# Remainders of all raw weight slabs by a negative ScalarE copy and an adding DMA, in a two-layer transformer kernel

## What is computed

```python
for i in range(DEPTH):
    x = layer_norm(DN_ALPHA * x + 0.5 * swiglu(x, ffn1_w_gate[i], ffn1_w_up[i], ffn1_w_down[i]), ...)
    y = swa_mixer(...) if kind == 0 else nsa_mixer(...)
    x = layer_norm(DN_ALPHA * x + y, ...)
    x = layer_norm(DN_ALPHA * x + mem_cross_attention(x, mem, ...), ...)
    x = layer_norm(DN_ALPHA * x + 0.5 * swiglu(x, ffn2_w_gate[i], ffn2_w_up[i], ffn2_w_down[i]), ...)
```

## Time and profile before

| | before |
|---|---|
| median of 3 runs | 2184.62 us (2184.2 to 2186.59) |
| profiled execution | 2184.3 us from its first to its last instruction |
| TensorE busy | 2161.4 us (99%) |
| VectorE busy | 1334.5 us (61%) |
| ScalarE busy | 1068.6 us (49%) |
| GpSimd busy | 779.0 us (36%) |
| HBM traffic | 203.10 MB read, 2.10 MB written, 94 GB/s |

### The profile page before, as it was taken

One profiled execution on the slowest core, in us unless ns is written; L12 is line 12 of the kernel. 1 busy time (PEld: TensorE's weight loads), 2 busy tenths in 40 slices (PEclk: granted clock), 3 DMA queues, 4 the chain that ended last, 5 costly groups with the idle time before them and its releaser, 6 DMA issues.

```text
span 2184.3 us, 35402 instructions
## 1 busy us (share of the span) xinstructions
PE 2161.4 (99%) x13640; PEld 1918.4 (88%) x13640; DVE 1334.5 (61%) x2315; ACT 1068.6 (49%) x1927; POOL 779.0 (36%) x573
## 2 busy tenths in 40 slices
PE   9999999999999999999999999999999999999998
PEld 8999998878888989898899999887778887989896
DVE  7656667464436928385766666657655346747475
ACT  4434345563435525254643534466654445535353
POOL 3201116567638030305420111555548555120203
PEclk9999999999999999999999999999999999999999
DMA  4323334213313333333232333320004312333332
GB/s 152 122 93 95 110 113 134 77 49 109 123 39 107 107 97 108 95 110 123 87 118 96 97 107 114 119 79 29 20 11 132 110 49 77 116 97 96 108 97 78
DMA packets 58199, 207.50 MB, mean 95 GB/s; under 512 B 6960, under 2 KB 7088, under 8 KB 57264
## 3 DMA queue, kind: packets, MB, share of 16 engines
q1 hardware_dynamic: 56016, 197.68, 28.9%
q10 hardware_dynamic: 2016, 7.55, 0.9%
HBM read 203.10 MB, written 2.10 MB: 94 GB/s over the span
## 4 chain that ended last, share of the span: by engine, by line
PE 93%; DVE 3%; ACT 1%; POOL 1%; issue 1%; DMA 0%; DVEq 0%; ACTq 0%
PE bank L1772 14%; PE bank L1773 14%; PE bank L1774 14%; PE bank L1983 11%; PE bank L1988 11%; PE bank L1985 11%; PE bank L2184 2%; PE bank L2145 2%; PE bank L2117 1%; PE bank L2118 1%; PE bank L1872 1%; PE bank L1874 1%; PE bank L1873 1%; PE bank L1791 1%; PE bank L1802 1%
## 5 line engine op out<-in xcount | busy, mean ns | idle before, releaser
L627 POOL TENSOR_TENSOR w_lo<-w_raw,w_hi 128x1024 fp32r<-128x1024 f32 (+1 forms) x226 | 530.1, 2354 | 1175.3 <-ACT w_hi L804 1175.2
L1772 PE MATMUL bank<-h_hi,w_hi 128*128 128x512 f32 x960 | 377.8, 394 | 1.5 <-DVE h_lo L1751 0.8
L1773 PE MATMUL bank<-h_lo,w_hi 128*128 128x512 f32 x960 | 374.4, 390 | 0.0
L1774 PE MATMUL bank<-h_hi,w_lo 128*128 128x512 f32 x960 | 373.8, 389 | 0.0
L804 ACT ACTIVATE w_hi<-w_raw 128x1024 fp32r<-128x1024 f32 (+1 forms) x227 | 230.4, 1021 | 130.5 <-PE bank L1774 92.4
L1772 PEld LDWEIGHTS bank<-h_hi,w_hi 128*128 128x128 f32 x960 | 180.3, 188 | 45.5 <-issue 3.3
L1774 PEld LDWEIGHTS bank<-h_hi,w_lo 128*128 128x128 f32 x960 | 180.2, 188 | 38.2
L1773 PEld LDWEIGHTS bank<-h_lo,w_hi 128*128 128x128 f32 x960 | 180.5, 188 | 34.2
L1983 PE MATMUL bank<-x_hi,w_hi 128*128 128x256 f32 x864 | 139.6, 284 | 0.3
L1772 PE MATMUL bank<-x_hi,w_hi 128*128 128x512 f32 x352 | 139.2, 396 | 0.0
L1988 PE MATMUL bank<-x_hi,w_lo 128*128 128x256 f32 x864 | 138.9, 283 | 0.0
(11 more groups left out here) (307 smaller groups left out, 5036.0 us busy)
## 6 DMA issues: line engine op xcount, KB each, us to landing
w_raw<-w_dram SPq DMA_DIRECT2D x315, 512.0 KB, 3.5
w_raw<-w_dram SPq DMA_DIRECT2D x64, 448.0 KB, 3.3
f<-mem_dram ACTq DMA_DIRECT2D x5, 1024.0 KB, 5.2
out_dram<-t SPq DMA_DIRECT2D x8, 256.0 KB, 2.2
t<-x_dram SPq DMA_DIRECT2D x2, 512.0 KB, 6.9
f<-cmp_w_dram ACTq DMA_DIRECT2D x1, 1024.0 KB, 4.9
t<-x_dram ACTq DMA_DIRECT2D x2, 256.0 KB, 5.5
t<-x_dram ACTq DMA_DIRECT2D x1, 512.0 KB, 8.1
```

The costliest lines, as they stand in the source:

```text
L627: pool.tensor_tensor(w_lo[:, slot(s), 0:n * P], w_raw[:, s % RAW, 0:n * P], w_hi[:, slot(s), 0:n * P].bitcast(F32), ALU.subtract).then_inc ...
L1772: pe.matmul(dst, w_hi[:, slot(s), w], m_hi[:, k, :], start=k == 0, stop=False)
L1773: pe.matmul(dst, w_hi[:, slot(s), w], m_lo[:, k, :], start=False, stop=False)
L1774: last = pe.matmul(dst, w_lo[:, slot(s), w], m_hi[:, k, :], start=False, stop=k == n - 1)
```

## The change

ScalarE now writes two copies of a raw slab: the rounded one into w_hi as before, and right behind it one with scale -1 into w_lo, which then holds minus the rounded value. GpSimd issues a DMA that reads the same slab from DRAM a second time and adds it onto w_lo (`accum_op=ALU.add`), so that w_lo ends as the remainder. This replaces GpSimd's subtraction for 226 slabs, and VectorE's `gate_rest` and `up_rest` for the 76 gate slabs and 76 up halves of the Strassen groups. The remainders of sums (`pair_rest`, `late_rest`) and of slab 0 stay with VectorE. neg_ready counts the negative copies; lo_landed (one for each slot), gate_lo and up_lo now count landings, 16 for each. SyncE reloads a raw buffer after the negative copy. To make room for the new semaphores iota_done is merged into pool_set and sinks_neg into dist_ready; their waits (pool_set at 8 and 9, dist_ready at 6) are not all shown.

```diff
         hi_ready = sem("hi_ready")
-        lo_ready = sem("lo_ready")
+        neg_ready = sem("neg_ready")
+        lo_landed = [sem(f"lo_landed{i}") for i in range(SLOTS)]
...
+        row_of = {}
+        for n in set(sizes):
+            for row, s in enumerate([s for s in range(total) if sizes[s] == n]):
+                row_of[s] = row
+
+        def turn_of(s):
+
+            return len([x for x in range(s + 1) if x not in grouped and x not in by_dve and slot(x) == slot(s)])
+
+        turns_of = {s: turn_of(s) for s in range(total)}
...
         def wait_lo(engine, s):
 
-            before = len([x for x in by_dve if x < s])
             if s in by_dve:
-                engine.wait_ge(lo_dve, before + 1)
+                engine.wait_ge(lo_dve, by_dve.index(s) + 1)
             else:
-                engine.wait_ge(lo_ready, plain(s) - before)
+                engine.wait_ge(lo_landed[slot(s)], 16 * turns_of[s])
...
             for s, n in enumerate(sizes):
                 if s >= RAW and s - RAW in grouped:
                     g = grouped[s - RAW]
                     if s - RAW == g.gate:
-                        sp.wait_ge(gate_lo, g.count + 1)
+                        sp.wait_ge(gate_hi, 2 * g.count + 2)
                         sp.wait_ge(wsum_ready, 4 * g.count + 4)
                     else:
                         sp.wait_ge(wsum_ready, 4 * g.count + 2)
-                        sp.wait_ge(up_lo, g.count + 1)
+                        sp.wait_ge(up_hi, 2 * g.count + 2)
+                elif s >= RAW and s - RAW in by_dve:
+                    wait_lo(sp, s - RAW)
                 elif s >= RAW:
-                    wait_lo(sp, s - RAW)
+                    sp.wait_ge(neg_ready, plain(s - RAW) - len([x for x in by_dve if x < s - RAW]))
...
-                sp.dma_start(w_raw[:, s % RAW, 0:n * P], io["w%d" % n][rows[n], :, :]).then_inc(raw_landed[s % RAW], 16)
-                rows[n] += 1
+                sp.dma_start(w_raw[:, s % RAW, 0:n * P], io["w%d" % n][row_of[s], :, :]).then_inc(raw_landed[s % RAW], 16)
...
-                    pool.wait_ge(hi_ready, plain(s))
-                    pool.tensor_tensor(w_lo[:, slot(s), 0:n * P], w_raw[:, s % RAW, 0:n * P],
-                                       w_hi[:, slot(s), 0:n * P].bitcast(F32), ALU.subtract).then_inc(lo_ready, 1)
+                    pool.wait_ge(neg_ready, plain(s) - len([x for x in by_dve if x < s]))
+                    pool.dma_start(w_lo[:, slot(s), 0:n * P], io["w%d" % n][row_of[s], :, :],
+                                   accum_op=ALU.add).then_inc(lo_landed[slot(s)], 16)
...
+            def group_rests(g):
+
+                pool.wait_ge(gate_hi, 2 * g.count + 2)
+                if g.count:
+                    pool.wait_ge(gate_lo, 16 * g.count)
+                pool.dma_start(w_gate(g)[1], io["w8"][row_of[g.gate], :, :], accum_op=ALU.add).then_inc(gate_lo, 16)
+                pool.wait_ge(up_hi, 2 * g.count + 2)
+                if g.count:
+                    pool.wait_ge(up_lo, 16 * g.count)
+                pool.dma_start(w_up(g)[1], io["w8"][row_of[g.up], :, 512:1024], accum_op=ALU.add).then_inc(up_lo, 16)
...
             def ffn(st):
                 feed(st.up[0][WHOLE - 1][1])
                 if st.ln == 0:
                     masks()
                 for part in range(len(FPARTS)):
-                    feed(st.out[part][-1])
+                    for g in st.groups[part]:
+                        if g is not st.groups[0][0] and g is st.groups[part][0]:
+                            feed(st.out[part - 1][-1])
+                        group_rests(g)
+                feed(st.out[-1][-1])
                 if st.ln in MEMORY:
                     memory_split(MEMORY[st.ln])
                 feed(st.out[-1][-1] + 3)
...
@@ -802,6 +826,9 @@
                         act.wait_ge(slab_done, plain(same_slot(s)))
                     after_group(s)
                     act.activation(w_hi[:, slot(s), 0:n * P], w_raw[:, s % RAW, 0:n * P], ACT.Copy).then_inc(hi_ready, 1)
+                    if s not in by_dve:
+                        act.activation(w_lo[:, slot(s), 0:n * P], w_raw[:, s % RAW, 0:n * P], ACT.Copy,
+                                       scale=-1.0).then_inc(neg_ready, 1)
...
                     act.activation(w_gate(g)[0], raw(g.gate), ACT.Copy).then_inc(gate_hi, 1)
+                    act.activation(w_gate(g)[1], raw(g.gate), ACT.Copy, scale=-1.0).then_inc(gate_hi, 1)
...
                     act.activation(w_up(g)[0], raw_half(g.up, 1), ACT.Copy).then_inc(up_hi, 1)
+                    act.activation(w_up(g)[1], raw_half(g.up, 1), ACT.Copy, scale=-1.0).then_inc(up_hi, 1)
...
-            dve.wait_ge(iota_done, 3)
+            dve.wait_ge(pool_set, 8)
...
-                def gate_rest(g):
-
-                    dve.wait_ge(gate_hi, g.count + 1)
-                    hi, lo = w_gate(g)
-                    dve.tensor_tensor(lo, raw(g.gate), hi.bitcast(F32), ALU.subtract).then_inc(gate_lo, 1)
...
-                def up_rest(g):
-                    hi, rest = w_up(g)
-                    dve.wait_ge(up_hi, g.count + 1)
-                    dve.tensor_tensor(rest, raw_half(g.up, 1), hi.bitcast(F32), ALU.subtract).then_inc(up_lo, 1)
...
-                gate_rest(begin)
...
-                gate_rest(begin.next)
-                up_rest(begin)
...
                             sums_second(g.next)
-                            if g is not begin:
-                                gate_rest(g.next)
                             pair_rest(g.next)
...
-                        if g.next:
-                            up_rest(g.next)
...
                         elif after and j == 5:
-                            gate_rest(after)
                             pair_rest(after)
...
-                    if after:
-                        up_rest(after)
...
-                    pe.wait_ge(gate_hi, g.count + 1)
-                    quarter(bank_a(g)[:, 0:256], w_gate(g), 0, x_block(0, 0), True, (gate_lo, g.count + 1), m1)
+                    pe.wait_ge(gate_hi, 2 * g.count + 1)
+                    quarter(bank_a(g)[:, 0:256], w_gate(g), 0, x_block(0, 0), True, (gate_lo, 16 * g.count + 16), m1)
...
-                    quarter(bank_b(g)[:, half[1]], w_gate(g), 1, x_block(1, 0), True, (gate_lo, g.count + 1), m2)
+                    quarter(bank_b(g)[:, half[1]], w_gate(g), 1, x_block(1, 0), True, (gate_lo, 16 * g.count + 16), m2)
...
-                    pe.wait_ge(up_hi, g.count + 1)
+                    pe.wait_ge(up_hi, 2 * g.count + 1)
                     pe.wait_ge(up2_out, g.count + 1)
-                    quarter(bank_b(g)[:, half[0]], w_up(g), 0, comb[4], False, (up_lo, g.count + 1), m4)
```

More of the change, by code:

```diff
@@ L411, in build @@
         pool_set = sem("pool_set")
-        iota_done = sem("iota_done")
         dist_f = sem("dist_f")
@@ L418, in build @@
         cmp_in = sem("cmp_in")
-        sinks_neg = sem("sinks_neg")
         out_done = sem("out_done")
@@ L592, in _ @@
         def _(sp):
-            rows = {7: 0, 8: 0}
             for s, n in enumerate(sizes):
@@ L634, in _ @@
             pool.memset(eps[:], EPS).then_inc(pool_set, 1)
-            pool.iota(dist_i[:, 0:512], [[1, 512]], base=-384, channel_multiplier=-1).then_inc(iota_done, 1)
+            pool.iota(dist_i[:, 0:512], [[1, 512]], base=-384, channel_multiplier=-1).then_inc(pool_set, 1)
             pool.iota(dist_i[:, 512:640].rearrange("p (i n) -> p i n", i=NT), [[-128, NT], [16, 32]], base=0,
-                      channel_multiplier=-1).then_inc(iota_done, 1)
-            pool.iota(dist_i[:, 640:896], [[1, 256]], base=-128, channel_multiplier=-1).then_inc(iota_done, 1)
+                      channel_multiplier=-1).then_inc(pool_set, 1)
+            pool.iota(dist_i[:, 640:896], [[1, 256]], base=-128, channel_multiplier=-1).then_inc(pool_set, 1)
             pool.wait_ge(pool_set, 5)
@@ L655, in masks @@
                 pool.wait_ge(consts_in, 64)
-                pool.tensor_scalar(nsinks[:], sinks[:], -1.0, None, ALU.mult).then_inc(sinks_neg, 1)
+                pool.tensor_scalar(nsinks[:], sinks[:], -1.0, None, ALU.mult).then_inc(dist_ready, 1)
             def base(st, j):
@@ L710, in mixer @@
                     pool.wait_ge(x_ready, KC * (st.ln + 1))
-                    pool.wait_ge(sinks_neg, 1)
+                    pool.wait_ge(dist_ready, 6)
                     for p in range(2):
@@ L1638, in mixer @@
                 if st.kind == "swa":
-                    dve.wait_ge(sinks_neg, 1)
+                    dve.wait_ge(dist_ready, 6)
                 def recip(u):
@@ L1964, in shift @@
             def shift(st):
-                pe.wait_ge(pool_set, 6)
+                pe.wait_ge(pool_set, 9)
                 pe.wait_ge(lead_ready, st.ln + 1)
@@ L2018, in prod4 @@
                         pe.wait_ge(comb_lo, c0 + 3)
-                    pe.wait_ge(up_hi, g.count + 1)
+                    pe.wait_ge(up_hi, 2 * g.count + 1)
```

(2 more changed lines are left out.)

## The result

| | before | after |
|---|---|---|
| median of 4 runs | 2185.61 us (2184.2 to 2187.03) | 2568.14 us (2558.68 to 2579.24) |
| profiled execution | 2184.3 us | 2564.9 us |

The ratio is 1.1753, 95% interval 1.1719 to 1.1786: slower by 382 us. The forecast was 2345 us, 160 us more than before, with a range up to 2540: the sign was right, the size was not.

The account below looks back on a forecast made before the run. TensorE was taken to bound the kernel, so only late w_lo counts: 2184.3 us + 152 of waits + 8 in layer norms = 2344, given as 2345 us against the runs' median; range 2235 to 2540.

Parts of the forecast that it names:

- the named places: Readers of w_lo with too short a gap: first down slabs, tight groups, output, memory and NSA input slabs; 152 us.
- One sign: GpSimd's busy time, listed among what would show the forecast right: POOL near 250 us.
- D = 5.5 us: Issue to landing of a 512 KB adding transfer into w_lo: 5.2 us from mem loads plus 0.3 us issue.
- the lower bound: D bounded from below by a plain 512 KB transfer: 3.5 us median, 3.0 us the fastest.
- the steady groups: The other 48 or so Strassen groups: gap 6.84 us, 0.3 us to spare, so no wait forecast.
- the first rival: Adding transfers land later, so steady groups wait too from D = 5.8 us; 2468 us at D = 7; chance 0.25.
- the sum had 51: Waits at tight Strassen groups: 30 us at first two groups of four stages, 21 at second groups of eight parts.
- the 16 places that the forecast named: Tight Strassen groups: first and second of four stages, second of eight later parts; 2.59 to 3.86 us each.
- 45 + 23 + 21 + 7 + 5 = 101: Waits outside groups: first down slabs 45, output slabs 23, memory pairs 21, NSA inputs 7, other places 5 us.
- rival 3: Waits of 3 to 4 us lower TensorE's clock: 58 us on the forecast, 2403 us; chance 0.12.
- 8 us were allowed: Layer norms: negative copies on ACT between x_hi copies; bounds 0 and 15 us, 8 taken.
- rival 1 at D = 8.1 us: Worst case of late landings: 111 us at 48 groups, 112 at 43 other places; 2570 us, 0.08, outside the range.

Follow-up runs that it names:

- e7: Kernel before, with only the 112 ordinary slabs whose w_hi lies ready 10 us or more taking the new route: 2196.02 us, ratio 1.0049.
- e9: e8 with one wait turned: SyncE reloads a gate's raw buffer when the adding transfer has landed, not after the negative copy: 2266.35 us, ratio 1.0365.
- e4: Changed kernel with plain transfers in place of adding ones, so w_lo holds the slab itself and only time is of use: 2335.7 us, ratio 1.0684.
- e8: Kernel before, with only the groups' gate remainders by negative copy and adding transfer; up halves by DVE, ordinary slabs by POOL: 2362.68 us, ratio 1.0798.
- e10: Changed kernel with SyncE reloading every raw buffer only when the adding transfer of its slab has landed: 2502.4 us, ratio 1.1453.
- e3: Kernel before plus ScalarE's negative copies; POOL and VectorE add w_raw onto them instead of subtracting, no adding transfer: 2231.15 us, ratio 1.0203.

## Why the prediction was wrong

**What bounds the kernel, and where it would hurt: right.** TensorE waits for adding transfers at the named places, and POOL's relief wins nothing that shows (`e7`); DVE's was not tested alone. One sign failed at no cost: POOL is busy for 570.5 us and not near 250, since each of its 378 issues counts 0.86 us.

**D = 5.5 us: right for a transfer alone, wrong for this kernel.** Lone landings took 5.64 us, the freed gates of `e9` 5.4 us. Without the addition a lone landing took 3.8 us (`e4`), between the 3.5 us of the lower bound and D, and over the 3.2 us that the prediction weighed for it. But the transfers are hardly ever alone, and the prediction put crowding into its range only. The step that failed has a sentence of its own: "SyncE loads the next raw slab after the negative copy rather than after the subtraction, 1.3 us earlier, for little". It looked at ACT's waits for raw slabs and not at what the load does to the adding transfer. That load now starts together with the adding transfer and shares its engines. It makes 5.4 us 6.7 (`e8` against `e9`), and with 0.3 us to spare in the steady groups that is the first rival: 60 waits and 111 us at L1996 where the sum had 51. With the raw load out of the way (`e9`) the groups wait 52.5 us, mostly at the 16 places that the forecast named.

**The ordinary slabs.** The first down slab of the 12 parts waits 5.36 us on average in place of 3.76 (19 us more in all); all readers but the groups have 150 us of waits where the sum had 45 + 23 + 21 + 7 + 5 = 101. In a down projection a slab is due each 5.4 us and its adding transfer alone takes that long, so it mostly has a raw load and another adding transfer beside it. The nine of `e10` without a raw load point to the raw load as what lengthens it; no run separates the two, as `e10` moved both.

**The clock: a rival that should have been a term.** The forecast kept "PE busy in us nearly unchanged" and gave rival 3 a chance of 0.12 and 58 us. It cost 119 us, 0.46 us for each us waited. Its estimate, one product of 1.44 us behind each of 40 waits, was too short: behind the wait at 112.73 the clock stays at half for 3.8 us and more, and 50 waits (15 of 1 to 3 us and all 35 longer ones) have such a stretch behind them.

**ScalarE: a term mis-sized.** 8 us were allowed, in the norms alone; `e3` shows 44.5, with 15 us of slower matmuls in it. Over half of it lies where ACT's copies out of the accumulators (first groups, NSA input) stand behind a negative copy, though the forecast had found room for the copies in the groups. In after it doesn't show by itself: TensorE's idleness rose by 261.5 us and the waits for w_lo are 261.6, so whatever ScalarE costs there lies inside them. Its share of the 109 us below was not separated.

**The sum.** 2344 forecast, 2565 found: 109 us more of waits (60 in the groups, 49 elsewhere), 119 of clock, and 8 that were allowed for the norms and don't show there: 2344 + 109 + 119 - 8 = 2564. Rivals 1 and 3 came together; each had been priced with the other at zero, and so the range ended below the time. That rival 1 at D = 8.1 us reads 2570 us, nearly the measured 2568, is luck: the landings had a median of 7.2 us, and 119 us of the loss are the clock.

## What to carry to other kernels

When a change moves a transfer's release, ask which other transfer the same event now releases: two that start together can lengthen each other, and the one that matters may miss its reader for that alone. Take a landing time from transfers that have company like yours. And where a forecast lets TensorE wait 3 us or more at a place, price the half clock behind it in the same term, here about half a us for each us waited. A route of 8.6 us (1.05 + 7.5, `e7`) costs next to nothing where there are 10 us of room, and what counts is the list of gaps, not the mean load.

## What the runs showed of the hardware

- An adding transfer of a slab (448 or 512 KB) from DRAM takes 5.4 to 5.6 us from issue to landing alone (medians of after, `e7`, `e9` and `e10`), the same without the addition 3.8 us (10 slabs of `e4`); SyncE's plain load took 3.5 us in before. The addition takes a packet from 150 to 286 ns of engine time (`e4` and after).
- With a raw load beside it from the start an adding transfer of a gate took 6.7 us (`e8`). With another adding one beside it and no raw load an ordinary slab took 5.3 to 5.8 us (nine slabs of `e10`).
- TensorE's granted clock went to half behind all 35 waits of 3 us and more, behind 15 of 36 of 1 to 3 us, and behind none of 43 shorter ones (after).
- POOL's issue is busy for 0.86 us with the addition and 0.53 us without (L636 in after and in `e4`), against 0.33 us of SyncE.
